# Products of the identity with itself, read by nobody, placed ahead of four waits of TensorE

## The chip, the core and the metric

The kernel runs on one core of a Trainium2 chip. Its engines are TensorE (PE: matrix products; its weight loads are listed as PEld), VectorE (DVE), ScalarE (ACT), GpSimd (POOL) and SyncE (SP), which issues the transfers. Each runs its own list of instructions in the order of the program, and they meet at semaphores. The metric is the device time of one execution in microseconds (us), smaller is better.

## What is computed

One inference step of a two-layer trunk, over 256 prompt tokens and 32 sample tokens (288 columns, `T`), model width 1024. Cut to what matters:

```python
h = layer_norm(x, ln_in_g, ln_in_b)
for l in range(2):
    y, ... = token_mixer(h, ...)            # one input projection, sparse attention, gated delta rule, merge, w_out
    h = layer_norm(ALPHA * h + y, ln1_g[l], ln1_b[l])
    if l % 2 == 0:
        f = (silu(h @ ffn_w1) * (h @ ffn_w3)) @ ffn_w2               # dense, 2816 wide
    else:
        gate = softmax of the top 2 of 8 router logits of h
        f = sum(gate[:, e] * swiglu(h, w1[e], w3[e], w2[e]) for e in range(8))   # 3584 wide
    h = layer_norm(ALPHA * h + f, ln2_g[l], ln2_b[l])
```

All data are float32.

## The kernel before

The program is a row of stages, each a `Block` in which every engine has a list of its own: `norm(0)`, then for each layer `front(l)` (the joined stage: projection, indexer, attention, convolution), `delta(l)` (gated delta rule), `merge(l)` (branches, output projection), and then `dense_mlp()` in layer 0 or `moe()` in layer 1; a last `norm` writes the output. At the end of a block the engines meet, and each jumps to its next list.

Activations stand transposed, as `hT` with 8 tiles of 128 channels by 288 tokens. Weights come in units of 1 MB through a ring of 6 slots that SP fills ahead. Two kinds of product occur. In `front`, the router and the sums, both operands are plain float32 (`ps<-hT,ring`, `ps<-hT,ones`). In the merge, the dense stage and the experts a weight unit is split by ScalarE (L375, `wh`) and VectorE (L381, `wl`) into a high and a low part in the rounded type float32r, the activations likewise (`hTh`, `hTl`), and three products of the parts take the place of one.

Between `merge` or `dense_mlp` and the stage behind it stands a LayerNorm over channels, spread over both blocks. TensorE ends a stage with `sum_products` (products with `ones` of the stream and of its square). In the next block ScalarE's `moments`, VectorE's `normalised`, GpSimd's `centred` and ScalarE's `scaled_out` (L660) make the new `hT` or `hTh` tile by tile, and TensorE's list begins with a wait for it (`h_ready`):

- `dense_mlp`: TensorE waits for the split of unit 1 and `h_ready`, then runs 64 products of `hTh` with the first two units, and then those of `hTl`, of which GpSimd makes the second half.
- `front(1)`: TensorE waits for its weight unit and, tile by tile, for `h_ready`, then runs a chunk of 80 columns and `wide` chunks of 128.
- `moe`: TensorE waits for the router's weights and `h_ready`, runs the router (24 float32 products of 8 columns, `ps<-experts,hT`), turns `hT` by 24 transposes (`ps<-ident,hT`), waits for VectorE's selection (`sel_ready`), counts positions (16 small products, up to L2459), waits for the one-hot matrices `oh` (L2349) and gathers expert 0's tokens: 8 tiles by 2 parts by 3 products of 128 columns (`ps<-oh,htokh`, `ps<-oh,htokl`). Behind it come the eight experts.

PSUM bank `ps[7]` is idle at the four places of the change: what was in it has been read, and what comes next is written with `start=True`.

Of the kernel before, what the change touches and what calls it, by code (L numbers as in the profile page):

```python
# [19 lines left out]
P = 128  # L20
# [53 lines left out]
def program(nc, A, OUT, upto=99):  # L74
    ctx = ExitStack()
    with ctx:
# [6 lines left out]
        ps = [ctx.enter_context(nc.psum_tensor(f"ps{b}", [P, 512], F32)) for b in range(8)]  # L83
# [10 lines left out]
        ident = sb("ident", [P, P])  # L94
# [18 lines left out]
        def layout(*tensors):  # L113
# [7 lines left out]
        cT, zT, arena, slopes, distr, identr, away, slopes4, identr4, _, oaT, obT = layout(  # L121
            ("cT", [P, CT, CO]),
            ("zT", [P, B_HEADS, T]), ("arena", [P, ARENA]),
            ("slopes", [P, A_HEADS, P], F32R),
            ("distr", [P, NT, PAST + DEC], F32R), ("identr", [P, P], F32R),
            ("away", [P, NT, PAST + DEC], F32R), ("slopes4", [P, 2, P], F32R), ("identr4", [P, P], F32R),
            ("pad", [P, OAB0 - CT * CO - B_HEADS * T - ARENA - A_HEADS * P - 2 * NT * (PAST + DEC) - 4 * P]), ("oaT", [P, 4, T]), ("obT", [P, 4, T]))
# [7 lines left out]
        _, tanhs = layout(("under", [P, GATE0]), ("tanhs", [P, 2 * KD, T]))  # L135
        DSM0 = GATE0 + 2 * KD * T
        _, dsm = layout(("below_small", [P, DSM0]), ("dsm", [P, OAB0 - DSM0]))
# [5 lines left out]
        _, yT = layout(("splits", [P, 2 * WS * SLOT]), ("yT", [P, KD, T]))  # L143
# [6 lines left out]
        _, htokl = layout(("above", [P, 2 * WS * SLOT + 2 * KD * CAP + 2 * (D_FFE // P) * CAP]), ("htokl", [P, NT, D], F32R))  # L150
# [70 lines left out]
        def slot(n, dims):  # L221
            s = (n % RING) * SLOT
            size = 1
            for d in dims:
                size *= d
            v = ring[:, s:s + size]
            return v.rearrange("p (a b) -> p a b", a=dims[0])
# [156 lines left out]
        def halves(n, dims):  # L384

            k = split_index(n) % WS
            return [w[:, k, :].rearrange("p (a b) -> p a b", a=dims[0]) for w in (wh, wl)]

        def have_split(pe, n, experts=0):
            pe.wait_ge(unit_used, n + 1 + N_EXP * experts)  # L390
# [155 lines left out]
        def norm(call, j, g_vec=None, b_vec=None, final=False):  # L546

            gb = gb_all
            with nc.Block() as block:  # L549
                @block.sync  # L550
                def _(sp):
                    if not final:
                        load_units(sp, 0, 3)
                        return
                    sp.dma_start(gb[:, 0, :], g_vec.partition_broadcast(P)).then_inc(gb_in, 16)  # L555
                    sp.dma_start(gb[:, 1, :], b_vec.partition_broadcast(P)).then_inc(gb_in, 16)
                    for i in range(2):
                        sp.wait_ge(hat_ready, NT * call + i + 1)
                        sp.dma_start(OUT["y_prompt"][0, P * i:P * i + P, :], resid[:, i, :]).then_inc(out_stored, 16)
                    sp.wait_ge(hat_ready, NT * (call + 1))  # L560
                    sp.dma_start(OUT["y_sample"][0], resid[0:DEC, 2, :]).then_inc(out_stored, 16)
                    sp.wait_ge(out_stored, 48)

                @block.vector
                def _(dve):
                    c = chain(dve, "dve")
                    for i, (t0, n) in enumerate(TILES):
                        for a in range(2):
                            c(nc.vector.bn_stats(stats[0:n, i, a, :], resid[0:n, i, 512 * a:512 * a + 512]))
                    for i, (t0, n) in enumerate(TILES):  # L570
                        c.sync() if i == 0 else None
                        c(nc.vector.bn_aggr(mv[0:n, i, :], stats[0:n, i, :, :].rearrange("p a b -> p (a b)")))
                    c.sync()
                    nc.vector.tensor_scalar(rstd[:], mv[:, :, 1], LN_EPS, None, ALU.add).then_inc(var_ready, 1)
                    if final:

                        dve.wait_ge(gb_in, 32)
                        for i, (t0, n) in enumerate(TILES):
                            c(nc.vector.scalar_tensor_tensor(out=resid[0:n, i, :], in0=resid[0:n, i, :], scalar=mv[0:n, i, 0:1],  # L579
                                                             in1=gb[0:n, 0, :], op0=ALU.subtract, op1=ALU.mult))  # L580
                    dve.wait_ge(std_ready, call + 1)
                    c.link(nc.vector.reciprocal(rstd[:], std[:]))  # L582
                    for i, (t0, n) in enumerate(TILES):
                        if final:
                            ins = nc.vector.scalar_tensor_tensor(out=resid[0:n, i, :], in0=resid[0:n, i, :], scalar=rstd[0:n, i:i + 1],  # L585
                                                                 in1=gb[0:n, 1, :], op0=ALU.mult, op1=ALU.add)
                        else:
                            ins = nc.vector.tensor_scalar(resid[0:n, i, :], resid[0:n, i, :], mv[0:n, i, 0:1],
                                                          rstd[0:n, i:i + 1], ALU.subtract, ALU.mult)
                        ins.then_inc(hat_ready, 1)  # L590
                    for k in range(1, 0 if final else KD, 2):
                        dve.wait_ge(nrm_turned, k + 1)
                        nc.vector.tensor_scalar(hT[:, k, :], ps[k][:, 0:T], lnp[:, 2 * j, k:k + 1],
                                                lnp[:, 2 * j + 1, k:k + 1], ALU.mult, ALU.add)
                    keep(c, "dve")

                @block.scalar
                def _(act):
                    act.wait_ge(var_ready, call + 1)
                    nc.scalar.activation(std[:], rstd[:], ACT.Sqrt).then_inc(std_ready, 1)  # L600
                    for k in range(0, 0 if final else KD, 2):
                        act.wait_ge(nrm_turned, k + 1)
                        nc.scalar.activation(hT[:, k, :], ps[k][:, 0:T], ACT.Identity,
                                             bias=lnp[:, 2 * j + 1, k:k + 1], scale=lnp[:, 2 * j, k:k + 1])

                @block.tensor
                def _(pe):
                    for k in range(0 if final else KD):
                        for i, (t0, n) in enumerate(TILES):
                            if k == 0:  # L610
                                pe.wait_ge(hat_ready, i + 1)
                            ins = nc.tensor.transpose(ps[k][:, t0:t0 + P], resid[:, i, P * k:P * k + P], ident[:])
                        ins.then_inc(nrm_turned, 1)
# [6 lines left out]
        LNP = [1, 2, 3]  # L620
        EPS = [1, 0, 1]
        XC_DVE = 4

        def sum_products(pe, q, m):

# [137 lines left out]
        def front(l):  # L763
# [25 lines left out]
            with nc.Block() as block:  # L789
# [50 lines left out]
                def _(pe):  # L840
# [155 lines left out]
                    def turn_out_sample():  # L996
                        pe.wait_ge(orow_ready, l * NT + 3)
                        nc.tensor.transpose(ps[7][:, 0:P], orow[:, 0:P], ident[:]).then_inc(o_turned, 1)

                    sw = slot(u0, (8, 80))  # L1000
                    have(pe, u0)
                    for k in range(KD):
# [1039 lines left out]
        def dense_mlp():  # L2042
            n0 = first["mlp", 0]
            with nc.Block() as block:
# [13 lines left out]
                @block.tensor  # L2058
                def _(pe):
                    w0 = [halves(n0 + u, (8, 256)) for u in range(2)]  # L2060
                    have_split(pe, n0 + 1)
                    for k in range(KD):
                        pe.wait_ge(h_ready, k + 1)
# [146 lines left out]
        def moe():  # L2210
            iu = itmp
            with nc.Block() as block:
# [205 lines left out]
                @block.gpsimd  # L2418
                def _(pool):
                    centred(pool, 2)  # L2420
                    pool.wait_ge(xc_ready, 3 * (KD - XC_DVE))
                    for j, h in enumerate((htokh, htokl)):
                        nc.gpsimd.memset(h[DEC:2 * DEC, 2, :].bitcast(F32), 0.0).then_inc(tail_zero, 1)
                        pool.wait_ge(tail_zero, 2 * j + 1)
                        nc.gpsimd.memset(h[2 * DEC:P, 2, :].bitcast(F32), 0.0).then_inc(tail_zero, 1)
                        pool.wait_ge(tail_zero, 2 * j + 2)
# [8 lines left out]

                @block.tensor
                def _(pe):
                    pe.wait_ge(lgt_in, 16)
                    for k in range(KD):
                        pe.wait_ge(h_ready, 2 * KD + k + 1)  # L2440
# [17 lines left out]
                    for i, (t0, n) in enumerate(TILES):  # L2458
                        ins = nc.tensor.matmul(ps[6][:, 32:32 + NE], ones[0:n, :], selm[0:n, i, :], start=(i == 0), stop=(i == NT - 1))  # L2459
                    ins.then_inc(pos_done, 1)  # L2460
                    pe.wait_ge(pos_ready, 1)
                    pe.wait_ge(oh_ready, 1)
                    pe.wait_ge(tail_zero, 4)
# [205 lines left out]
```

## Time and profile before

| | us |
|---|---|
| median of 3 runs | 2050.94 |
| lowest and highest | 2050.41 and 2051.27 |
| profiled execution | 2051.66 |
| its span, first to last instruction | 2049.9 |
| busy TensorE / VectorE / ScalarE | 1953.1 / 1356.7 / 1062.4 |
| mean granted TensorE clock | 0.976 of full speed |

The span is that of the profiled execution; 1.8 us of its own time lie around it. The granted clock has two levels, 1.0 (2.4 GHz) and 0.5 (1.2 GHz). Busy time of TensorE is made of modelled ends, so in what follows the cost of a product is read from one start to the next. A line such as `x2` in the timeline joins neighbouring records of one kind, and "[8.25 <-ACT hTh L660]" is idle time ahead of the row and what ended it.

### The profile page before, as it was taken

How to read it: one execution, taken by the hardware profiler on the slowest of the kernel's cores; microseconds unless marked ns; L12 is line 12 of the kernel's file. 1: busy time of each engine (PE TensorE's matmuls, PEld its weight loads, DVE VectorE, ACT ScalarE, POOL GpSimd, SP SyncE). 2: the span in 40 equal slices, each digit the busy share in tenths (PEclk: the TensorE clock that was granted, in tenths of full speed). 3: DMA queues.
4: the chain of work that ended last, by engine and by line, in shares of the span. 5: the costliest groups of instructions: out<-in, count | busy, mean ns of one | idle time of the engine just before them, and what ended most of it. 6: DMA issues, size and time to landing. Idle time of an engine off the chain costs nothing. (4 is left out here: it accounts for less than half of the span.)

```text
span 2049.9 us, 25915 instructions
## 1 busy us (share of the span) xinstructions
PE 1953.1 (95%) x10571; PEld 1644.5 (80%) x10571; DVE 1356.7 (66%) x1548; ACT 1062.4 (52%) x1206; POOL 84.9 (4%) x149
## 2 busy tenths in 40 slices
PE   6999998899989999988899999999999999999995
PEld 5677878899976778878788888888888888888884
DVE  3744136644434643255497987979879798797986
ACT  2233224444323323233576776767767677676773
POOL 4002000200011011000000000000000000000000
PEclk9999999999999999999699999999999999999998
DMA  7222235255431332243299999999999999899992
GB/s 203 83 86 92 63 89 167 91 178 165 151 91 62 103 110 70 60 137 108 97 373 344 333 373 300 376 341 336 372 300 374 341 337 373 301 375 340 331 380 107
DMA packets 260479, 456.89 MB, mean 223 GB/s; under 512 B 32218, under 2 KB 111274, under 8 KB 260356
## 3 DMA queue, kind: packets, MB, share of 16 engines
q1 hardware_dynamic: 258966, 454.74, 64.8%
q8 instruction: 86, 1.41, 0.3%
q10 hardware_dynamic: 1390, 0.44, 0.1%
q14 instruction: 37, 0.30, 0.0%
HBM read 452.11 MB, written 3.04 MB: 222 GB/s over the span
## 5 line engine op out<-in xcount | busy, mean ns | idle before, releaser
L381 DVE TENSOR_TENSOR wl<-ring,wh 128x2048 fp32r<-128x2048 f32 x385 | 880.6, 2289 | 256.5 <-ACT wh L375 253.2
L375 ACT ACTIVATE wh<-ring 128x2048 fp32r<-128x2048 f32 x385 | 737.1, 1917 | 321.4 <-PE ps L350 321.4
L350 PE MATMUL ps<-hT,ring 128*128 128x288 f32 (+1 forms) x1376 | 360.2, 414 | 9.2 <-ACT hT L660 8.3
L350 PE MATMUL ps<-wh,xgh 128*128 128x512 f32 x896 | 355.0, 396 | 2.2 <-DVE wl L381 2.2
L350 PE MATMUL ps<-wh,xgl 128*128 128x512 f32 x896 | 349.9, 390 | 0.0
L350 PE MATMUL ps<-wl,xgh 128*128 128x512 f32 x896 | 349.6, 390 | 0.0
L350 PEld LDWEIGHTS ps<-hT,ring 128*128 128x128 f32 (+1 forms) x1376 | 254.0, 190 | 83.0 <-issue 15.2
L350 PEld LDWEIGHTS ps<-wh,xgh 128*128 128x128 f32 x896 | 168.6, 188 | 40.0 <-DVE wl L381 5.6
L350 PEld LDWEIGHTS ps<-wh,xgl 128*128 128x128 f32 x896 | 168.5, 188 | 36.1
L350 PEld LDWEIGHTS ps<-wl,xgh 128*128 128x128 f32 x896 | 168.7, 188 | 33.4
L350 PE MATMUL ps<-wh,gEh 128*128 128x512 f32 x448 | 143.5, 401 | 0.0
L350 PE MATMUL ps<-wl,gEh 128*128 128x512 f32 x448 | 139.6, 393 | 0.0
L350 PE MATMUL ps<-wh,gEl 128*128 128x512 f32 x448 | 138.1, 390 | 0.0
L350 PE MATMUL ps<-hTh,wh 128*128 128x288 f32 x352 | 105.1, 300 | 8.2 <-ACT hTh L660 8.2
L350 PE MATMUL ps<-hTh,wl 128*128 128x288 f32 x352 | 104.2, 298 | 0.0
L350 PEld LDWEIGHTS ps<-wh,gEl 128*128 128x128 f32 x448 | 84.1, 188 | 19.3
L350 PEld LDWEIGHTS ps<-wl,gEh 128*128 128x128 f32 x448 | 84.0, 188 | 18.9
L350 PE MATMUL ps<-hTl,wh 128*128 128x288 f32 x352 | 98.7, 295 | 0.0
L350 PEld LDWEIGHTS ps<-wh,gEh 128*128 128x128 f32 x448 | 78.9, 189 | 12.1
L1749 ACT ACTIVATE arena<-ps 128x512 f32<-128x512 f32 (+1 forms) x72 | 32.4, 491 | 103.7 <-PE ps L1566 67.8
L350 PEld LDWEIGHTS ps<-hTh,wh 128*128 128x128 f32 x352 | 67.4, 191 | 8.7 <-issue 8.7
L1566 PEld LDWEIGHTS ps<-arena 128*128 128x128 f32 (+1 forms) x672 | 64.3, 163 | 6.4
(404 smaller groups left out, 2424.6 us busy)
## 6 DMA issues: line engine op xcount, KB each, us to landing
ring<-in_moe_w SPq DMA_DIRECT2D x336, 1024.0 KB, 5.4
ring<-in_w_in SPq DMA_DIRECT2D x38, 1024.0 KB, 5.2
ring<-in_ffn_w SPq DMA_DIRECT2D x33, 1024.0 KB, 5.2
ring<-in_w_out SPq DMA_DIRECT2D x8, 1024.0 KB, 5.3
ring<-in_w_in SPq DMA_DIRECT2D x32, 128.0 KB, 3.0
ring<-in_w_oa SPq DMA_DIRECT2D x16, 256.0 KB, 4.0
ring<-in_w_ob SPq DMA_DIRECT2D x8, 512.0 KB, 5.0
resid<-in_x_prompt SPq DMA_DIRECT2D x1, 1024.0 KB, 5.3
```

The lines of the kernel that those rows point to most:

```text
L350: ins = nc.tensor.matmul(*a, **k)
L375: nc.scalar.activation(wh[:, k % WS, :], ring[:, s:s + SLOT], ACT.Copy).then_inc(hi_ready, 1)
L381: nc.vector.tensor_tensor(wl[:, k % WS, :], ring[:, s:s + SLOT], wh[:, k % WS, :].bitcast(F32), ALU.subtract).then_inc(unit_used, 1)
L1566: return nc.tensor.matmul(v4(b, n, ww)[:, h, :], d[lhs][0:n, h, :], d[rhs][0:n, h, :], start=True, stop=True)
L1749: nc.scalar.activation(tl[i][dst][0:n], v4(bank(r, i), n, BD if r == "u" else n), ACT.Copy).then_inc(prep_act, 1)
```

## The change

A helper issues a given number of products on TensorE: the float32 identity `ident` as the stationary operand, and the same identity read four times over (512 columns) as the moving one, into `ps[7]`. They wait for nothing and signal nothing. 17 of them stand first in TensorE's list of `dense_mlp`, of `moe` and of `front(1)`; 4 more stand in `moe` between the position counts and the wait ahead of the gather. At the other calls the number is 0.

```diff
+        def idle_products(times):
+
+            for _ in range(times):
+                nc.tensor.matmul(ps[7][:], ident[:], ident[:].unsqueeze(1).to_broadcast([P, 4, P]), start=True, stop=True)
...
+                    idle_products(17 if l else 0)
                     sw = slot(u0, (8, 80))
                     have(pe, u0)
...
                     w0 = [halves(n0 + u, (8, 256)) for u in range(2)]
+                    idle_products(17)
                     have_split(pe, n0 + 1)
...
+                    idle_products(17)
                     pe.wait_ge(lgt_in, 16)
...
                     ins.then_inc(pos_done, 1)
+                    idle_products(4)
                     pe.wait_ge(pos_ready, 1)
                     pe.wait_ge(oh_ready, 1)
```

On TensorE, at the passage from the merge of layer 0 to the dense stage (the branches are the block's end and the jump to the next list):

```order
 L350 MATMUL ps<-hT,ones 128x288
 L350 MATMUL ps<-resid,ones 128x288
-L1944 UNCONDITIONAL_BRANCH
-L2058 UNCONDITIONAL_BRANCH
+L1951 UNCONDITIONAL_BRANCH
+L2065 UNCONDITIONAL_BRANCH
+L628 MATMUL ps<-ident 128x512 x17
 L350 MATMUL ps<-hTh,wh 128x288
 L350 MATMUL ps<-hTh,wl 128x288
```

The 17 products stand behind the jump, so ahead of the first `hTh` product and of the waits that it carries.

On TensorE, in the expert stage, from the transposes of `hT` to the gather:

```order
 L350 MATMUL ps<-ident,hT 128x128 x8
 L350 MATMUL ps<-ident,hT 32x128 x4
...
+L2468 MATMUL ps<-experts,ones 128x8 x3
+L628 MATMUL ps<-ident 128x512 x4
 L350 MATMUL ps<-oh,htokh 128x128 x3
 L350 MATMUL ps<-oh,htokl 128x128 x3
```

The four stand between the last position count and the first gather; nothing else moved on any engine.

## Rows read from the trace of the kernel before

**Rows 1.** The page: TensorE's busy us; its granted clock, 40 slices, tenths.

```profile
PE 1953.1 (95%) x10571; PEld 1644.5 (80%) x10571; DVE 1356.7 (66%) x1548; ACT 1062.4 (52%) x1206; POOL 84.9 (4%) x149
PEclk9999999999999999999699999999999999999998
```

**Rows 2.** Waits of TensorE: total us, times, longest.

```profile
PE ps L350 <- ACT hT L660: 16.5, 2, 8.3
```

**Rows 3.** Timeline, TensorE, into the dense stage: start us, us, instructions, count.

```profile
374.13 0.65 PE L350 MATMUL ps<-hT,ones 128*128 128x288 f32 x2
...
375.58 0.65 PE L350 MATMUL ps<-resid,ones 128*128 128x288 f32 x2
384.48 0.58 PE L350 MATMUL ps<-hTh,wh 128*128 128x288 f32 x1 [8.25 <-ACT hTh L660]
...
389.34 0.30 PE L350 MATMUL ps<-hTh,wh 128*128 128x288 f32 x1
389.47 0.29 PE L350 MATMUL ps<-hTh,wl 128*128 128x288 f32 x1
```

**Rows 4.** Stretches: busy us per engine, then granted clock, DMA share, GB/s.

```profile
390.00:605.00 215.00, 214.45 (x1590) 212.74 (x1589) 94.36 (x88) 79.86 (x85) 5.39 (x3) 1.00 0.48 149
...
376.00:379.00 3.00, 0.23 (x1) 0.00 (x0) 2.02 (x3) 1.25 (x3) 1.68 (x2) 1.00 0.43 101
379.00:389.00 10.00, 4.52 (x19) 4.55 (x20) 9.97 (x19) 5.29 (x9) 2.90 (x4) 0.50 0.55 181
...
605.00:611.00 6.00, 1.04 (x5) 0.48 (x3) 4.21 (x5) 1.25 (x3) 3.87 (x5) 1.00 0.28 73
611.00:618.00 7.00, 3.71 (x8) 2.14 (x9) 5.45 (x11) 4.25 (x8) 6.06 (x12) 0.51 0.01 0
...
978.00:988.00 10.00, 9.62 (x50) 9.26 (x51) 2.38 (x10) 3.86 (x8) 0.92 (x1) 0.50 0.02 5
...
993.00:996.00 3.00, 2.08 (x19) 1.89 (x18) 2.86 (x12) 3.00 (x7) 0.00 (x0) 0.94 0.01 3
997.00:1008.00 11.00, 10.00 (x47) 10.03 (x48) 2.62 (x10) 1.32 (x3) 0.00 (x0) 0.50 0.00 0
```

**Rows 5.** Timeline, TensorE, into the joined stage of layer 1.

```profile
605.39 0.65 PE L350 MATMUL ps<-resid,ones 128*128 128x288 f32 x2
614.29 9.75 PE L350 MATMUL ps<-hT,ring 128*80 128x288 f32 x32 [8.25 <-ACT hT L660]
623.97 0.23 PE L1011 MATMUL ps<-ident,arena 16*128 16x16 f32 x1
```

**Rows 6.** Timeline, TensorE, a passage between blocks with no data to wait for.

```profile
769.73 1.13 PE L350 MATMUL ps<-hT,ring 128*128 128x288 f32 x4
771.62 1.13 PE L1584 MATMUL ps<-arena,ones 128*128 128x128 f32 x8 [0.75 <-PEq L789]
```

**Rows 7.** Groups by form, TensorE: count, busy us, mean ns of one record.

```profile
L350 PE MATMUL ps<-hT,ones 128*128 128x288 f32 x48 | 15.6, 406 | 0.0
```

**Rows 8.** Timeline, TensorE, the head of the expert stage.

```profile
978.38 9.32 PE L350 MATMUL ps<-experts,hT 128*128 128x8 f32 x48 [8.25 <-ACT hT L660]
987.63 5.38 PE L350 MATMUL ps<-ident,hT 128*128 128x128 f32 x24
993.83 0.39 PE L2456 MATMUL ps<-experts,before 128*128 128x8 f32 x2 [0.82 <-DVE experts L2569]
...
994.97 0.93 PE L2459 MATMUL ps<-experts,ones 128*128 128x8 f32 x6
998.00 0.87 PE L350 MATMUL ps<-oh,htokh 128*128 128x128 f32 x3 [2.11 <-DVE oh L2349]
...
1008.27 0.73 PE L350 MATMUL ps<-wh,xgh 128*128 128x512 f32 x1
1008.81 0.63 PE L350 MATMUL ps<-wl,xgh 128*128 128x512 f32 x1
```

**Rows 9.** Timeline, TensorE, a later gather amid the down products.

```profile
1097.88 0.50 PE L350 MATMUL ps<-oh,htokl 128*128 128x128 f32 x3
1098.22 0.68 PE L350 MATMUL ps<-wh,gEh 128*128 128x512 f32 x2
```

More of the change, by code:

```diff
@@ L607, in _ @@
                 def _(pe):
+                    idle_products(0 if final else 0)
                     for k in range(0 if final else KD):
```

## The prediction

> **What bounds the kernel now.** I read the page first. TensorE is busy for 95% of the span and no other engine for more than 66%, and the row of the granted clock is 9 all along but for one slice of 6 [rows 1]. So TensorE is the bound, and the reader should ask where it stands idle or runs at half clock. The waits say where it stands: 16.5 us in two waits for `hT`, one of them at the head of the joined stage of layer 1, the other at the head of the expert stage [rows 2], and 8.25 us for `hTh` at the head of the dense stage [rows 3]. All three are the same LayerNorm, made by ACT, DVE and POOL while TensorE has nothing to do. The stretches then say what the idleness costs beyond itself: TensorE enters it at full clock (376 to 379 us: 1.00), the clock falls to 0.50 at 379 and is back at 389, and the dense stage behind it is filled to 214.45 of 215 us at clock 1.00 [rows 4]. The last figure matters most for this change: behind the place where the new products go, TensorE has no idle time left in which a late start could be made up.
>
> **When an added product can run.** The products stand behind a block's end. The row that shows a bare passage between blocks: two float32 products start at 769.73 and take until 770.70, and the next block's first product starts at 771.62, so 0.92 us pass [rows 6]. The last sum product of the merge starts at 375.58 [rows 3]; with 0.48 us for itself and 0.92 for the passage the first new product starts at 376.98. The wait that it stands ahead of ends at 384.48. So the room is 7.5 us, and the same in the joined stage (605.39 + 1.40 = 606.8 against 614.29) [rows 5] and, by the same 8.25 us of idle time, in the expert stage [rows 8].
>
> **What one costs.** No row of before shows a float32 product of 512 columns that isn't in the rounded type. The nearest are the sums with `ones`: the group counts 48 records for 24 calls of the helper (8 tiles, three LayerNorms), so a plain float32 product is two records [rows 7], and three of them stand between 374.13 and 375.58, 0.483 us each for 288 columns at full clock [rows 3]. The cost grows with the columns, so for 512 I take 0.483 x 512 / 288 = 0.86 us. The other end of the price is that of a single record, half of that, 0.43 us, which would hold if this product were made in one record as the transposes are (24 transposes, 24 records) [rows 8]. I take 0.86, since both operands are plain float32 and it isn't a transpose; all plain float32 products I looked at come in pairs. At this price 17 products take 14.6 us at full clock: twice the room.
>
> The Trainium skill (TensorE: Matmul & The Clock Gate, "Back-to-back issue gap") gives about 216 ns for 512 columns at full clock, without a word on the type. By it 17 products would take an estimated 3.7 us and fit with room to spare; the trace disagrees for this type, with 0.483 us for 288 columns [rows 3].
>
> **Dense stage.** The new products run from 376.98 to 391.6, so the first real product starts 7.1 us later than 384.48. Against that, the clock has not fallen: between 384.48 and 389.34 stand 20 products of 288 columns (0.24 each), which at full clock take 0.133 each (389.34 to 389.47), 2.7 us for 4.9 [rows 3]: 2.2 saved. Net +4.9. Nothing hides it: TensorE is full until 605 [rows 4], and the other engines only wait for it.
>
> **Joined stage of layer 1.** Again +7.1. 32 records, 16 products, run from 614.29 to 623.97, 9.7 us [rows 5]; at 0.483 each they would take 7.7, since the clock stays up. Saved 2.0, net +5.1. Later waits of TensorE in this stage are for ACT's and DVE's answers to its own products and move with it.
>
> **Expert stage.** The router starts 7.1 us later, at 985.5. At half clock [rows 4] it took 9.25 us, 978.38 to 987.63 [rows 8], so 4.6 at full. In the rows of before the clock never rose during it, so it will fall again behind the new products, as it did 3 us behind the last sum product at 376.1 and 5 us behind that at 605.9 [rows 4, 5]. With a fall after 4 us the router ends at 990.7, +3.1 (bounds +2.5 if it never falls, +4.2 if it falls after 2.9). From the router's end to the first position count 6.2 us pass, mostly DVE and ACT, 987.63 to 993.83 [rows 8], and the counts take 1.9: they end at 995.8 now, at 998.9 then. The four new products take 3.4 us at full clock, 6.9 at half. The transposes ahead of them lift the clock (0.94 in 993 to 996), and the thin stretch behind lets it fall again (0.50 from 997) [rows 4]: I take 5.2. They end at 1004.1, where the one-hots would have allowed 1001.1. The gather's 48 products took 10.3 us at half clock (998.00 to 1008.27); a later gather gives 0.11 each at full clock, three in 0.34 [rows 9], so 5.3 in all. It ends at 1009.4 for 1008.3, +1.1; and the products behind it, 0.54 us apart at first (1008.27 to 1008.81), ran at half clock for some 2 us, of which 1.0 is saved. Net +0.1. Bounds: -2.3 (router +2.5, four products at full clock) and +2.9 (router +4.2, four at half clock); if the gather also runs at half clock, +9. In the rows of before 10 us of gather, 998 to 1008, didn't lift the clock [rows 4], so the last is possible.
>
> The Trainium skill (TensorE: Matmul & The Clock Gate, "Part 4: PE-mode transpose") says that the high clock doesn't engage for transposes. By it the four products would always start at half clock, which adds at most 1.7 to the above; the trace disagrees, since the clock stood at 0.94 of full in 993 to 996, right behind 24 transposes [rows 4] [rows 8].
>
> **Sum.** 4.9 + 5.1 + 0.1 = +10.1 us. The profiled execution took 2051.66, 0.7 above the median; against it the sum gives 2061.8, against the median 2050.94 it is 2061.0.
>
> **Rivals.** A, the cheap product (faster). If a new product is one record of 0.43 us, 17 take 7.3 and end at 384.3, just ahead of 384.48. Then the dense stage only gains 2.2 and the joined stage 1.9. In the expert stage the router starts in time and mostly at full clock, ends near 983.7 (-3.9), and the gather starts at about 994.4 and takes between 5.3 and 10.3, say 7.8: -6.1. Together -10.2: 2040.7. For it: 17 x 0.43 matches the room almost exactly. Against it: the paired records of every plain float32 product [rows 7]. The point that decides is the price: each 0.1 us on it costs 51 x 0.1 = 5.1 us over the three places, so that gain turns to loss near 0.64 us, well off both 0.43 and 0.86. The rounded type is cheaper still (0.54 us for 512 columns at half clock [rows 8], so about 0.25 at full): at that price 17 end at 381.2, 3.3 us before the wait does, the clock holds or falls, and the time lies between A's and no change; I count it here. It is about what the skill's figure amounts to. 9% in all.
>
> B, the clock isn't held: identity operands are nearly all zeros, and if such products don't keep it up, it falls 3 us in and the remaining 13.5 products cost 1.73 each, 23 us, with nothing saved behind: +18.9 at each of three places and +4.7 at the four, 2112. Against it: the transposes, with the identity as an operand, lifted the clock. 3%.
>
> C, the delay is taken up: something other than TensorE ends last behind the places, so that 6 or more of the 10.1 us vanish, about 2053. It would need idle time on TensorE that isn't an answer to its own work; the 214.45 of 215 speak against it, and the transfers are loaded ahead. 6%.
>
> **How the numbers follow.** The forecast has 82%. Its own bounds: the passage between blocks could be nothing (-0.9 at each of three places) and the expert stage -2.3: +5.0, 2056; at the top the gather at half clock, +19, 2070. The range 2055 to 2070 holds nearly all of this case and little of the others. A measurement of this kernel can tell about 0.2%, 4.1 us, from no change: slower is the forecast and B, 0.85; within is C, 0.06; faster is A, 0.09.
>
> **What would show it.** In the profile of the changed kernel: 34 records, not 17, for the new products in the dense stage, 0.43 us apart; TensorE's 8.25 us waits gone and its first real product at about 391.6, with ACT's `hTh` long done; clock 1.00 throughout 376 to 400. The joined stage's first product, 12 us later than now, is at 626.3. In the expert stage the gather at 0.11 a product; the clock low in part of the router or of the four. Wrong would be: 17 records (A), a fall to 0.50 within the new products (B), or new idle time of TensorE later in the dense or joined stage (C).

## The result and the profile after

The changed kernel takes 2059.85 us, median of 6 runs (2059.66 to 2060.49), against 2051.14 us for the kernel before on the same chip (6 runs, 2050.41 to 2052.53). The ratio is 1.004 with a 95% interval of 1.0028 to 1.0053: slower by 8.7 us (the interval is 5.7 to 10.9), where +10.1 was forecast. The profiled execution took 2060.49 us, its span is 2058.8.

TensorE's waits for `hT` and `hTh` [rows 2, 3] are gone, and the mean granted clock rose from 0.976 to 0.988. So the change does what it says, and the kernel is slower for it. First the page of the changed kernel, the lines that answer to rows 1 (busy us and share; granted clock in 40 slices), and then, from its groups by form, that of the new products (count, busy us, mean ns of one record, idle time before them):

```profile
PE 1987.7 (97%) x10681; PEld 1653.6 (80%) x10681; DVE 1356.0 (66%) x1548; ACT 1062.4 (52%) x1206; POOL 85.0 (4%) x149
PEclk9999999999999999999999999999999999999998
```

```profile
L628 PE MATMUL ps<-ident 128*128 128x512 f32 x110 | 49.9, 612 | 1.0 <-PEq L1951 0.6 <-PEq L2051 0.3
```

110 records for 55 products: two to a product. In what follows the head of a stage is the start of TensorE's list in it. The timeline of TensorE into the dense stage (start us, us, what, count), which answers to rows 3:

```profile
374.03 0.65 PE L350 MATMUL ps<-resid,ones 128*128 128x288 f32 x2
375.00 14.83 PE L628 MATMUL ps<-ident 128*128 128x512 f32 x34 [0.32 <-PEq L1951]
389.26 0.69 PE L350 MATMUL ps<-hTh,wh 128*128 128x288 f32 x1
389.80 0.29 PE L350 MATMUL ps<-hTh,wl 128*128 128x288 f32 x1
...
392.31 0.29 PE L350 MATMUL ps<-hTh,wh 128*128 128x288 f32 x1
```

The second real product starts 15.8 us behind the last sum product (389.80 - 374.03); before it was 9.3 (384.86 - 375.58). The 21st, the one at which the clock was back before (389.34 - 375.58 = 13.8), comes after 18.3. So of the later start about 2.0 us had been won back by then. GpSimd's `hTl` tiles, done at 393.8 here, hold up nothing: this profile has no wait for them.

The joined stage of layer 1 (rows 5) and the head of the expert stage (rows 8), TensorE's timeline:

```profile
608.47 0.65 PE L350 MATMUL ps<-resid,ones 128*128 128x288 f32 x2
609.44 14.83 PE L628 MATMUL ps<-ident 128*128 128x512 f32 x34 [0.32 <-PEq L2051]
624.11 7.92 PE L350 MATMUL ps<-hT,ring 128*80 128x288 f32 x32
631.97 0.23 PE L1018 MATMUL ps<-ident,arena 16*128 16x16 f32 x1
...
977.53 0.65 PE L350 MATMUL ps<-resid,ones 128*128 128x288 f32 x2
...
993.17 5.90 PE L350 MATMUL ps<-experts,hT 128*128 128x8 f32 x48
999.00 5.38 PE L350 MATMUL ps<-ident,hT 128*128 128x128 f32 x24
1005.20 0.39 PE L2465 MATMUL ps<-experts,before 128*128 128x8 f32 x2 [0.82 <-DVE experts L2579]
...
1007.20 5.40 PE L628 MATMUL ps<-ident 128*128 128x512 f32 x8
1012.03 0.85 PE L350 MATMUL ps<-oh,htokh 128*128 128x128 f32 x3
...
1017.74 0.45 PE L350 MATMUL ps<-wh,xgh 128*128 128x512 f32 x1
```

And the granted clock (the third number from the end of each line) in four stretches there, the router, its tail with the transposes, the four new products, and the gather:

```profile
993.00:998.00 5.00, 5.00 (x44) 4.54 (x42) 0.00 (x0) 0.00 (x0) 0.00 (x0) 1.00 0.00 0
998.00:1005.00 7.00, 6.38 (x32) 5.41 (x30) 2.39 (x22) 4.82 (x9) 0.00 (x0) 0.51 0.01 4
...
1008.00:1012.00 4.00, 4.00 (x7) 1.54 (x5) 2.93 (x12) 0.00 (x0) 0.00 (x0) 0.57 0.00 0
1012.00:1018.00 6.00, 6.00 (x51) 5.74 (x50) 0.00 (x0) 1.49 (x3) 0.00 (x0) 1.00 0.00 0
```

With the last sum product ahead of each head as the mark, the difference of the two profiled executions comes apart so:

| stretch, by TensorE's starts | before, us | after, us | difference | forecast |
|---|---|---|---|---|
| start to the last sum product ahead of the dense stage | 375.58 | 374.03 | -1.55 | 0 |
| dense stage, to the last sum product of the next head | 229.81 | 234.44 | +4.63 | +4.9 |
| joined stage of layer 1, delta and merge | 364.09 | 369.06 | +4.97 | +5.1 |
| expert stage to its first expert product | 38.79 | 40.21 | +1.42 | +1.1 |
| the rest | 1041.63 | 1041.06 | -0.57 | -1.0 |
| span | 2049.9 | 2058.8 | +8.9 | +10.1 |

Nothing of the change runs in the first stretch, so its -1.55 needed a run of its own.

### The profile page after: what moved, and what is told of

Same layout as the page of the kernel before. It is cut to its first block and busy times, and to the rows that moved or that the text cites. A ratio compares the mean times of both kernels' runs of the same rounds, so it can differ in the third digit from the quotient of the medians.

```text
span 2058.8 us, 26135 instructions
## 1 busy us (share of the span) xinstructions
PE 1987.7 (97%) x10681; PEld 1653.6 (80%) x10681; DVE 1356.0 (66%) x1548; ACT 1062.4 (52%) x1206; POOL 85.0 (4%) x149
## 5 line engine op out<-in xcount | busy, mean ns | idle before, releaser
L350 PEld LDWEIGHTS ps<-hTh,wl 128*128 128x128 f32 x352 | 66.3, 188 | 0.2 <-issue 0.2
```

The costliest lines, as they stand in the source:

```text
L350: ins = nc.tensor.matmul(*a, **k)
```

## The experiments

Each is told by its edit, the record of what was expected, and what came. The time of the kernel before was taken anew on the chip of each group: 2052.01 for the first four, 2052.45 for the next three, 2051.46 for the last. Single runs of one kernel lie 5 to 6 us apart in these groups, and 10 us in one of them, so small differences are read from the stages of the profiled executions, where equal stages with the same falls of the clock agree within about 0.2 us.

**The kernel before once more.** No edit.

> The kernel before, unchanged, profiled once more. In its first profile the last sum product of layer 0's merge starts at 375.58 us, in that of the changed kernel at 374.03, though nothing of the change runs before that. Theory 1 (where a fall of the clock lands differs from execution to execution, and the first profile had a stretch at half clock near 51 us that the other hadn't): this profile may show any of the two, and where it has no such stretch the row stands near 374.0. Theory 2 (the longer instruction list of the changed kernel moved it): 375.6 again, with the stretch at half clock in its place.

It took 2050.49 us, and the first stretch was shorter than in the first profile. In the new profile, TensorE's timeline near 51 us and at the end of that stretch, and the stretch of 51 to 55 us (busy time, then the granted clock, third from the end):

```profile
51.89 1.13 PE L893 MATMUL ps<-arena 64*128 64x256 f32 x8 [1.26 <-ACT arena L1148]
57.03 1.13 PE L893 MATMUL ps<-arena 64*128 64x256 f32 x8
...
374.27 0.65 PE L350 MATMUL ps<-resid,ones 128*128 128x288 f32 x2
```

```profile
51.00:55.00 4.00, 3.11 (x17) 2.39 (x17) 3.01 (x7) 1.83 (x4) 0.00 (x0) 1.00 0.01 2
```

And the same places in the first profile:

```profile
51.18 2.00 PE L893 MATMUL ps<-arena 64*128 64x256 f32 x8 [1.26 <-ACT arena L1148]
...
57.97 1.13 PE L893 MATMUL ps<-arena 64*128 64x256 f32 x8
```

```profile
51.00:55.00 4.00, 3.82 (x13) 2.66 (x14) 2.50 (x6) 1.12 (x3) 0.00 (x0) 0.57 0.01 2
```

Theory 1 held: in the unchanged kernel, too, the stretch can be 1.31 us shorter (375.58 - 374.27) of the 1.55. A fall of the clock in the indexer's score products (L893) costs 1.65 us by itself: from the second group of them to the third 6.79 us pass in the first profile and 5.14 in the new one. The new profile had reached that place 0.7 us later, and won 0.4 us more in the merge. It is scatter of the program, not the change.

**8 products at each head in place of 17.**

```diff
-                    idle_products(17 if l else 0)
+                    idle_products(8 if l else 0)
...
-                    idle_products(17)
+                    idle_products(8)
...
-                    idle_products(17)
+                    idle_products(8)
```

> 8 new products at each of the three heads in place of 17, the 4 ahead of the gather kept. Theory 1 (each costs 0.86 us, they hold the clock, and 17 are simply too long for the room of 7.9 us): 8 take 6.9 us and end about 1 us before the wait does; dense stage -2.2, joined stage -2.0, expert stage 0.6 - 6.7 = -6.1, so -10.3 in all: 2040.8. Theory 2 (what is saved behind comes from the late start, by which ACT, DVE and POOL are ready, not from the clock): nothing is saved, 2049 to 2052. Theory 3 (an idle stretch of 1 us behind the new products is enough to lose the clock): the same, with clock 0.5 at the heads.

2048.75 us median, ratio to before 0.9979 (0.997 to 0.9989). So the sign turns with the number alone, which settles what made the change slower: the length of the row of new products. But the gain is 3.3 us and not 10.3. TensorE's timeline into the dense stage, and its waits there (total us, times, longest):

```profile
378.88 7.10 PE L628 MATMUL ps<-ident 128*128 128x512 f32 x16 [0.32 <-PEq L1951]
386.81 0.37 PE L350 MATMUL ps<-hTh,wh 128*128 128x288 f32 x1 [0.83 <-ACT hTh L666]
387.02 0.29 PE L350 MATMUL ps<-hTh,wl 128*128 128x288 f32 x1
...
397.00 0.40 PE L350 MATMUL ps<-hTl,wh 128*128 128x288 f32 x1 [0.67 <-POOL hTl L2062]
```

```profile
PE ps L350 <- POOL hTl L2062: 1.0, 2, 0.7
```

The first real product starts in time and at full clock (0.21 to the next), so the room and the price were right. But TensorE now reaches the `hTl` products early and waits for GpSimd, as it does nowhere in the profile of before. The dense stage took 229.32 us for 229.81: 0.5 won of 2.2. The joined stage's head, 607.23 to 624.19, took 16.96 for 18.58: 1.6 won of 2.0. In the expert stage the clock fell 1.5 us into the router (TensorE's timeline, then two stretches):

```profile
977.06 8.35 PE L350 MATMUL ps<-experts,hT 128*128 128x8 f32 x48 [0.83 <-ACT hT L666]
...
994.36 5.98 PE L628 MATMUL ps<-ident 128*128 128x512 f32 x8
```

```profile
978.00:979.00 1.00, 1.00 (x9) 0.96 (x9) 0.87 (x4) 1.00 (x3) 0.00 (x0) 0.76 0.04 14
979.00:988.00 9.00, 9.00 (x47) 8.46 (x48) 1.37 (x14) 3.05 (x7) 0.00 (x0) 0.50 0.00 1
```

The router took 8.3 us for 9.25, and the four products ahead of the gather ran mostly at half clock (5.4 us to the gather). From the last sum product to the first expert product 37.3 us pass for 38.8: 1.5 won, and 2.5 to the second expert's gather, where 6.1 were expected. So theory 1 is right on price, and on the clock in the dense and joined stages; it is wrong in its size where another engine comes next and, for the greater part, in the expert stage, where the clock did not hold through the router.

**17 in the expert stage alone.** By a slip in the edit this kernel has its 17 products at the head of the expert stage, not of the dense stage, and none elsewhere, the four ahead of the gather included. What was expected of it was written for the dense stage and doesn't apply; the run with 17 in the dense stage alone stands below.

```diff
-                    idle_products(17 if l else 0)
+                    idle_products(0 if l else 0)
...
-                    idle_products(17)
+                    idle_products(0)
...
                     idle_products(17)
                     pe.wait_ge(lgt_in, 16)
...
-                    idle_products(4)
+                    idle_products(0)
```

> The 17 new products at the head of the dense stage alone, none elsewhere. Theory 1 (their excess over the room, 6.7 us, less 2.1 saved by the clock, passes to the end in full, since TensorE has no idle time behind): +4.6, 2055.7, and the joined stage's wait 8.25 us as before. Theory 2 (part of it is made up later in the stage or at the next LayerNorm): below 2053.5.

2056.88 us, 4.9 above before, ratio 1.0022 (1.0012 to 1.0031). The dense stage took 229.7 us, as before. In the expert stage the router started 6.7 us later than before against the last sum product and ended 3.4 us later; that delay stood unchanged at the first expert product, 3.4 us late. The interval of the whole, 2.5 to 6.4 us, holds it; the 1.5 us between the two are not traced. TensorE's timeline:

```profile
968.09 0.65 PE L350 MATMUL ps<-resid,ones 128*128 128x288 f32 x2
969.06 14.83 PE L628 MATMUL ps<-ident 128*128 128x512 f32 x34 [0.32 <-PEq L1951]
983.73 6.03 PE L350 MATMUL ps<-experts,hT 128*128 128x8 f32 x48
989.68 5.38 PE L350 MATMUL ps<-ident,hT 128*128 128x128 f32 x24
```

**No products ahead of the gather, 17 at the heads.**

```diff
-                    idle_products(4)
+                    idle_products(0)
```

> 17 at the three heads, but none ahead of the gather. Theory 1 (the four cost 2.6 us of delay there and bring the gather from half to full clock): the gather starts 2.6 us earlier against the position counts, its 48 products take 10.3 us instead of 5.7, and the first expert products also run at half clock: 2.9 us more than with the four, 2062.8. Theory 2 (17 products at the head already leave the clock up as far as the gather): the gather at full clock without them, 2.6 less, 2057.3.

2064.78 us (4 runs), ratio 1.0061 (1.0045 to 1.0076), the slowest of all. Theory 1 held in its direction: from the last sum product to the first expert product 43.6 us pass, for 40.2 with the four, 3.4 more where 2.9 were expected. The gather's clock (a stretch, the granted clock third from the end) and its step in the timeline (0.64 us for three products) are those of the kernel before:

```profile
1011.00:1021.00 10.00, 10.00 (x47) 10.00 (x48) 1.68 (x3) 1.32 (x3) 0.00 (x0) 0.50 0.00 0
```

```profile
1019.99 0.84 PE L350 MATMUL ps<-oh,htokh 128*128 128x128 f32 x3
1020.63 0.84 PE L350 MATMUL ps<-oh,htokl 128*128 128x128 f32 x3
```

**17 in the dense stage alone.**

```diff
-                    idle_products(17 if l else 0)
+                    idle_products(0 if l else 0)
...
                     idle_products(17)
                     have_split(pe, n0 + 1)
...
-                    idle_products(17)
+                    idle_products(0)
...
-                    idle_products(4)
+                    idle_products(0)
```

> The 17 new products at the head of the dense stage alone, none elsewhere. Theory 1 (their excess over the room, less what the clock gives back, passes to the end in full): the dense stage 234.45 us between last sum products for 229.75, +4.7, as in the changed kernel, and the joined and expert stages as before; in all +4.7, 2.0 over the scatter. Theory 2 (part of it is made up at the next LayerNorm or behind): the following stages shorter than before by more than 1 us.

2057.25 us, 4.8 above before, ratio 1.0023 (1.0014 to 1.0032). The dense stage took 608.23 - 373.79 = 234.44 us, to 0.01 us that of the changed kernel, and the next head waits as it did:

```profile
608.23 0.65 PE L350 MATMUL ps<-resid,ones 128*128 128x288 f32 x2
617.13 10.07 PE L350 MATMUL ps<-hT,ring 128*80 128x288 f32 x30 [8.25 <-ACT hT L666]
```

Theory 1 held: the whole delay goes to the end. One stretch behind did come out shorter, the joined stage with its merge (362.8 us for 364.1 and 363.8 in the two profiles of before), mostly by a fall of the clock in the scores that this execution hadn't (0.5 near 645 us in both profiles of before); it is the same scatter as above.

**4 in the dense stage alone.**

```diff
-                    idle_products(17)
+                    idle_products(4)
                     have_split(pe, n0 + 1)
```

(and 0 at the other places).

> 4 new products at the head of the dense stage, none elsewhere: 3.4 us of work, then an idle stretch of 4.4 us before the first hTh product. Theory 1 (the clock falls only when TensorE has stood idle for about 3 us or more, as it did 2.9 us behind the last sum product): the clock may just fall at or before the first product, so a stretch at 0.5 there of 3 to 7 us, later than before; the stage gains 0 to 0.4. Theory 2 (any recent work is enough to hold it): clock 1.00 throughout and the same 229.3 us as with 8.

2050.67 us. TensorE stood idle for 4.26 us behind the four, and started at full clock all the same; the clock fell 1.1 us later, for 3.4 us. Its timeline, and two stretches there:

```profile
375.11 3.67 PE L628 MATMUL ps<-ident 128*128 128x512 f32 x8 [0.32 <-PEq L1951]
383.04 0.37 PE L350 MATMUL ps<-hTh,wh 128*128 128x288 f32 x1 [4.26 <-ACT hTh L666]
```

```profile
376.00:384.00 8.00, 3.74 (x14) 1.94 (x13) 7.97 (x12) 2.27 (x5) 3.56 (x4) 1.00 0.85 262
384.00:388.00 4.00, 4.00 (x21) 4.00 (x20) 4.00 (x11) 4.00 (x6) 1.34 (x2) 0.57 0.02 4
```

The stage took 603.49 - 374.14 = 229.35 us, the same as with 8 and the clock held throughout (229.32). That says the same as the waits for GpSimd: once TensorE starts in time, the clock in those 5 us is worth 0.5 us, not 2.2, since `hTl` comes last. By theory 1 the clock would fall at or before the first product; it fell a little later. Theory 2, that any recent work holds it, fell.

**8 at the heads, GpSimd relieved, and 6 at the head of both merges.** The edit is against the run with 8; the second argument names the PSUM bank.

```diff
+                    idle_products(6, 7)
                     for j in range(KD // 2):
...
-                    for k in range(XC_DVE, KD):
+                    for k in range(6, KD):
                         pool.wait_ge(h_ready, k + 1)
...
-                                    if k < XC_DVE:
+                                    if k < 6:
                                         pe.wait_ge(hl_dve, k + 1)
                                     else:
-                                        pe.wait_ge(hl_pool, k - XC_DVE + 1)
+                                        pe.wait_ge(hl_pool, k - 6 + 1)
...
-                    for k in range(XC_DVE):
+                    for k in range(6):
                         dve.wait_ge(h_ready, k + 1)
```

> 8 new products at the three heads and 4 ahead of the gather, as in the run with 8; in the dense stage VectorE makes six of the eight hTl tiles and GpSimd two (four and four before); and 6 new products at the head of both merges, where TensorE waits 6.7 us for the first split. Theory 1 (with 8 products the dense stage won only 0.4 us because TensorE, at full clock, caught up with GpSimd's hTl tiles and waited 1.0 us in two waits for them): the dense stage is 1.5 us shorter than in the run with 8, 227.8 us between the last sum products. The room in the merges is 5.3 us, since the block there begins only when VectorE's last obT is done; 24 products of the merge at 0.133 for 0.24 us: up to 2.6 less in each merge, if the splits of the next units don't end last. Sum up to -6.7 on the run with 8, about 2042. Theory 2 (the merge is bound by ACT's and DVE's splits of its first units, 2.3 us each on DVE): nothing won in the merges, about 2047.

2045.23 us (2040.58 to 2050.66, 7 runs), ratio to before 0.9961 (0.9947 to 0.9974): faster than both kernels, and short of the 2042 of theory 1. The dense stage took 602.24 - 373.50 = 228.74 us: 0.6 less than with 8 alone, where 1.5 was expected; TensorE still waits for `hTl`, 0.4 us for GpSimd's. The merge shows both theories at work. TensorE's timeline in the merge of layer 0:

```profile
305.12 5.39 PE L628 MATMUL ps<-ident 128*128 128x512 f32 x12 [1.40 <-PEq L1523]
310.44 0.40 PE L350 MATMUL ps<-oabh,wh 128*128 128x288 f32 x1
...
339.21 0.61 PE L350 MATMUL ps<-mTh,wh 128*128 128x288 f32 x1 [2.92 <-DVE mo_ L2027]
339.62 0.44 PE L350 MATMUL ps<-mTh,wl 128*128 128x288 f32 x1
```

The head runs at full clock and the `mTh` products begin 2.0 us earlier than in the kernel before, but they begin out of a wait of 2.9 us for VectorE and at half clock (0.41 and 0.24 to the next), and the merge ends only 0.4 to 0.8 us earlier. What is won ahead of a wait for another engine is partly spent in it. That the longer wait is what lost the clock (2.9 us, for 2.5 in every other merge) is not shown: in the run without products ahead of the gather the clock also fell in the `mTh` products of one merge, behind a wait of 2.5 us.

**4 ahead of the gather alone.**

```diff
-                    idle_products(17)
+                    idle_products(0)
                     have_split(pe, n0 + 1)
...
-                    idle_products(17)
+                    idle_products(0)
                     pe.wait_ge(lgt_in, 16)
```

(and 0 in the joined stage).

> The 4 new products ahead of the gather alone, none at the heads. Nothing before the position counts changes (they end 26.3 us behind the last sum product). Theory 1 (the four are worth their cost at this place whatever the heads do: they delay the gather but let it run at 0.11 in place of 0.21 us a product): they take 3.4 to 6.9 us, the gather begins 29.8 to 33 us behind the last sum product for 28.3, takes 5.7 for 10.3, and the expert products behind it start at full clock for 0.9 more: 1.5 to 4.5 us less than before in the expert stage. Theory 2 (they were worth it only behind the 17, which left the clock partly up): all four at half clock and the gather still at half clock, 3 us more than before.

2049.39 us against 2051.46, ratio 0.9988 (0.9979 to 0.9998). TensorE's timeline:

```profile
993.98 5.40 PE L628 MATMUL ps<-ident 128*128 128x512 f32 x8
998.81 0.85 PE L350 MATMUL ps<-oh,htokh 128*128 128x128 f32 x3
...
1000.50 0.50 PE L350 MATMUL ps<-oh,htokh 128*128 128x128 f32 x3
1000.83 0.50 PE L350 MATMUL ps<-oh,htokl 128*128 128x128 f32 x3
```

Theory 1 held. The gather begins 2.65 us later than before against the last sum product and takes 5.7 us for 10.3; the first expert product comes 1.9 us earlier and the second expert's gather 3.0 us earlier. The medians are 2.1 us apart, with an interval of 0.4 to 4.3, and single runs of the two kernels overlap. This is the part of the change that is worth having by itself.

## Why the prediction was right

**The price of a product** was the step on which the sign hung, and it held: 34 records, 0.43 us apart, 14.6 us for 17 products, as scaled from the pairs of 288 columns [rows 3, 7]. Rival A, one record each, and the cheaper price of the rounded type are out.

**The clock held** through the new products (1.00 from 376 to 400 us), so rival B is out: products of the identity with itself kept it up.

**The passage between blocks** was put at 0.92 us [rows 6] and is 0.49 here (374.51 to 375.00): that row stood for another passage, and what that one spent more on isn't shown. It made each of the three delays 0.4 us too long; the saving by the clock fell 0.2 us short in the two stages, which brings +4.9 to +4.63 and +5.1 to +4.97, within 0.1.

**Nothing hid the delay.** TensorE's full 215 us [rows 4] were the right thing to look at: the run with 17 in the dense stage alone puts the whole +4.7 at the end of that stage, and the time is 4.8 us longer. Rival C is out.

**The saving by the clock** had the right size in the changed kernel (2.0 for 2.2, and 1.8 for 2.0 in the joined stage), but the prediction took it for the clock's worth at this place, and that holds only because TensorE came so late. The run with 8 shows it: on time, TensorE meets GpSimd's `hTl` and keeps 0.5 of it. My forecast for 8 products, -10.3, was three times too large by this step (1.7 us) and more by another: some 3.6 us were missing in the expert stage (2.5 won to the second expert's gather, for 6.1), where the clock fell in the router and the four products ran mostly at half clock.

**The expert stage** was forecast +0.1 and is +0.85 (1.42 - 0.57). The mis-sized terms: the router at full clock was put at half of 9.25 us, and it is not. The three products of one of its 8 tiles take 0.70 us at full clock for 1.16 at half, so 5.6 in all. The clock fell 5.0 us behind the new products (4 were taken), so it took 5.8, and the router ended 3.3 us late for 3.1. The four products took 4.8 for 5.2, the gather 5.7 for 5.3. The products behind it won the 1.0 forecast: to the second expert's gather 88.4 us pass for 89.3. The other 0.4 us of the row "the rest" are within the scatter of that row: in the second profile of the kernel before it is 1042.2 us for 1041.6.

**The first stretch**, -1.55, was not in the sum and couldn't be: the profile of before had caught an execution with a fall of the clock in the scores. Against the medians, each of 6 runs, the change costs 8.7; without that stretch the two profiles say 10.4 (8.9 + 1.55). The interval of the measured difference, 5.7 to 10.9 us, holds both. What of the remaining 1.7 is scatter of other falls of the clock between single executions can't be told from these runs, so how near 10.1 comes to 8.7 is in part chance; what bears the forecast out is the stages.

The Trainium skill (TensorE: Matmul & The Clock Gate, "Why this matters for your kernels") asks to leave no long idle gaps between bursts of products, which speaks for filling them. The traces agree as far as the clock goes: it fell in each wait of 8.25 us and at no head of a dense or joined stage with 8 or 17 products in it. They don't as far as the time goes: with 17 the kernel is 8.7 us slower, and with 8 it is 3.3 us faster. Its sentence that the high clock doesn't engage for transposes (same page, "Part 4: PE-mode transpose") isn't borne out: in the changed kernel the clock was at 0.5 at 998 and back at 1.00 in 1005 to 1008, right behind 24 transposes.

## What to carry to other kernels

Work that only keeps an engine's clock up must be sized by its measured price for its own type, two records and 0.86 us for a plain float32 product of 512 columns here, since each microsecond beyond the room goes to the end where the engine is the bound: 17 cost 8.7 us, 8 won 3.3. Before counting the clock's gain, look for who is next: another engine that was just hidden by the slow start (GpSimd's `hTl` in the dense stage) takes most of it. By the stages, the place that won most here was the one where a long row of real work follows with nothing to wait for, the gather.

## What the runs showed of the hardware that I had not expected

- The two kinds of product scale differently with the clock. The router's products of 8 columns, in which loads of the stationary operand were busy for 9.26 of 10 us [rows 4], went from 1.16 to 0.70 us a tile, a factor of 0.60; products of 288 columns of float32 halve (0.24 for 0.48 us a record).
- The gather, whose 10 us at half clock never lifted it, kept the full clock for 5.7 us once it began at it (1.00 from 1012 to 1018). Whether the clock rises or stays is not the same question for the same work.
- After 4.26 us idle behind 3.4 us of work the clock was still full, and fell 1.1 us after TensorE had resumed; behind the sum products it fell after 2.9 us of idleness in one place and 5 in another [rows 4]. A fall can thus hit work that has already begun, and it moves the time of an unchanged kernel: the one in the score products by 1.65 us.
